# A fused two-block transformer kernel: zero multiplies on TensorE ahead of split features and variance squares, and modulation rows gathered in three batches

## The reference

```python
for l in range(DEPTH):                               # first block
    m_lat = (jax.nn.silu(c) @ ada_w[l] + ada_b[l])[:, None]
    m_ctx = jax.nn.silu(c_ctx) @ ada_w[l] + ada_b[l]
    sh1, sc1, g1, sh2, sc2, g2 = jnp.split(m_lat, 6, axis=-1)
    h_lat = rmsnorm(x, norm_g[l, 0]) * (1.0 + sc1) + sh1
    ...
    x = x + g1 * rmsnorm(y_lat, norm_g[l, 1])
    f_lat = swiglu(rmsnorm(x, norm_g[l, 2]) * (1.0 + sc2) + sh2, ffn_w_in[l], ffn_w_out[l])
    ...
for i in range(DEPTH):                               # second block
    x = layer_norm(DN_ALPHA * x + 0.5 * swiglu_2(x, ...), ...)
    y = mixer_ab(x, ...) if i % 2 == 0 else mixer_c(x, ...)
    x = layer_norm(DN_ALPHA * x + y, ...)
    x = layer_norm(DN_ALPHA * x + 0.5 * swiglu_2(x, ...), ...)
    x = x + jax.nn.sigmoid(x @ ple_wg[i] + ple_bg[i]) * (p[i] @ ple_wp[i])
```

## Time and profile before

| what | value |
|---|---|
| median of three executions | 2632.01 us |
| the profiled execution | 2630.2 us |
| its span, first to last instruction | 2628.4 us |
| TensorE busy (multiplies) | 2366.0 us, 90% of the span |
| VectorE, ScalarE, POOL busy | 1277.7, 894.1, 120.1 us |
| mean granted clock of TensorE | 0.945 of full speed |
| chain of waits | TensorE 84%, VectorE 10%, ScalarE 3% |
| weight stream | 346 loads of 1024 KB |

### The profile page before, as it was taken

The page is one execution under the profiler, slowest core; times in us unless marked ns, Lnnn a source line. Parts: engine busy times, 40 slices in busy tenths (PEclk is TensorE's granted clock), DMA queues, the critical chain, the costliest instruction groups (busy, mean ns, idle before and its releaser), DMA issues.

```text
span 2628.4 us, 39106 instructions
## 1 busy us (share of the span) xinstructions
PE 2366.0 (90%) x17300; PEld 2181.0 (83%) x17300; DVE 1277.7 (49%) x1457; ACT 894.1 (34%) x929; POOL 120.1 (5%) x68
## 2 busy tenths in 40 slices
PE   7988888998899788999799878998899898888997
PEld 5876755998899556999799868998799795878996
DVE  4246425554454243544544545544554586526444
ACT  4212313334333132333433334333333434124332
POOL 0037400000000000000000000000000020000000
PEclk9988998999999999999899989999899996999998
DMA  7246701554355121355355313543354350013451
GB/s 304 98 164 262 289 16 60 180 188 160 133 187 177 71 88 64 144 184 184 128 185 177 129 69 126 188 176 142 130 186 181 108 182 16 1 66 135 177 188 35
DMA packets 52481, 373.10 MB, mean 142 GB/s; under 512 B 5728, under 2 KB 6752, under 8 KB 7840
## 3 DMA queue, kind: packets, MB, share of 16 engines
q1 hardware_dynamic: 51584, 367.78, 38.4%
q0 software_dynamic: 800, 3.93, 0.4%
HBM read 370.64 MB, written 1.05 MB: 141 GB/s over the span
## 4 chain that ended last, share of the span: by engine, by line
PE 84%; DVE 10%; ACT 3%; POOL 1%; issue 1%; DMA 1%; SPq 0%; DVEq 0%; ACTq 0%; POOLq 0%
PE PS L342 10%; PE PS L343 10%; PE PS L344 10%; PE PS L189 7%; PE PS L357 6%; PE PS L356 6%; PE PS L355 6%; PE PS L298 4%; PE PS L645 2%; DVE ring_r L443 2%; PE PS L280 2%; PE PS L263 2%; PE PS L265 2%; PE PS L264 2%; PE PS L281 2%; PE PS L282 2%
## 5 line engine op out<-in xcount | busy, mean ns | idle before, releaser
L443 DVE TENSOR_TENSOR ring_r<-ring,AR_r 128x2048 fp32r<-128x2048 f32 x274 | 625.0, 2289 | 605.8 <-ACT AR_r L437 595.4
L437 ACT ACTIVATE AR_r<-ring 128x2048 fp32r<-128x2048 f32 x274 | 520.1, 1908 | 705.4 <-PE PS L357 306.2
L342 PE MATMUL PS<-AR_r 128*128 128x256 f32 x2240 | 635.3, 284 | 0.0
L343 PE MATMUL PS<-AR_r 128*128 128x256 f32 x2240 | 634.7, 283 | 0.0
L344 PE MATMUL PS<-AR_r,ring_r 128*128 128x256 f32 x2240 | 634.6, 283 | 0.0
L342 PEld LDWEIGHTS PS<-AR_r 128*128 128x128 f32 x2240 | 430.9, 192 | 0.0
L343 PEld LDWEIGHTS PS<-AR_r 128*128 128x128 f32 x2240 | 430.9, 192 | 0.0
L344 PEld LDWEIGHTS PS<-AR_r,ring_r 128*128 128x128 f32 x2240 | 430.9, 192 | 0.0
L355 PE MATMUL PS<-AR_r 128*128 128x256 f32 x1232 | 348.7, 283 | 0.0
L356 PE MATMUL PS<-AR_r 128*128 128x256 f32 x1232 | 348.7, 283 | 0.0
L357 PE MATMUL PS<-AR_r,ring_r 128*128 128x256 f32 x1232 | 348.6, 283 | 0.0
(11 more groups left out here) (346 smaller groups left out, 3290.8 us busy)
## 6 DMA issues: line engine op xcount, KB each, us to landing
ring<-stream SPq DMA_DIRECT2D x346, 1024.0 KB, 4.8
X<-xt SPq DMA_DIRECT2D x1, 2048.0 KB, 10.1
AR<-bias POOLq DMA_DIRECT2D x1, 1536.0 KB, 6.8
AR<-pt POOLq DMA_DIRECT2D x2, 512.0 KB, 3.8
out<-X SPq DMA_DIRECT2D x1, 1024.0 KB, 4.8
SM<-small SPq DMA_DIRECT2D x1, 545.0 KB, 4.1
AR<-invc SPq DMA_DIRECT2D x1, 512.0 KB, 15.3
X<-negl POOLq DMA_DIRECT2D x1, 512.0 KB, 4.0
```

The lines of the kernel that those rows point to most:

```text
L342: pe.matmul(o, w_hi, X_HI[:, k, :], start=(k == 0), stop=False)
L343: pe.matmul(o, w_hi, X_LO[:, k, :], start=False, stop=False)
L437: act.activation(W_HI[i % 3], ring[:, n % SLOTS, :], ACT.Identity).then_inc(split_hi, 1)
L443: dve.tensor_tensor(RING_R[:, n % SLOTS, :], ring[:, n % SLOTS, :], W_HI[i % 3], ALU.subtract).then_inc(split_lo, 1)
```

## The change

It has two parts.

1. `pe_idle_turns` multiplies the zero tile by itself (128 x 128, float32, start and stop) a number of times into a bank that the next work overwrites. 24 such multiplies stand at the head of `pe_chunks_as_features_come`, ahead of its waits, for every tag but `ffn4`; that is nine places: `ffn0_lat`, `ffn0_ctx`, `ffn1_lat`, `ffn2`, `ffn3`, `ple2`, `mix3_in`, `ffn5`, `ple3`. Six stand in `pe_norm` ahead of its first wait for six tags (all in `pe_layernorm`).
2. The 24 groups of modulation are gathered in three batches (4, 8 and 12 groups), each in one PSUM bank: a group's columns of `CS` are shifted by a window so that its two results land on rows of their own, and all groups of a batch accumulate. One copy by ScalarE and one turn (4 multiplies with 8, 16 or 24 columns) serve a batch. The copies and turns of the single groups go: 24 copies become 3, 24 turns become 3.

```diff
@@ pe_norm
             bank = norm_bank(cols) if bank is None else bank
+            if tag in ("ffn2", "mix2", "ffn3", "ffn4", "mix3", "ffn5"):
+                pe_idle_turns(pe, bank, 6)
             for k in range(DT):
...
@@ modulation
-        ada_bank = lambda g: g % 3
+        ADA_BATCHES = [range(0, ADA_FIRST), range(ADA_FIRST, 12), range(12, ADA_GROUPS)]
...
         def pe_ada_rows(pe, g):
+            b = batch_of(g)
+            row = 2 * (g - ADA_BATCHES[b][0])
+            if row == 0:
+                pe.matmul(PS[:, b, 0:2], ZERO[:, :], ZERO[:, 0:2], start=True, stop=False, skip_group_check=True)
             for c in range(2):
...
                 need_chunk(pe, n)
-                if g >= 3 and c == 0:
-                    pe.wait_ge(S["ada_taken"], S.at("ada_taken", g - 3))
                 for k in range(DT):
                     strip = slice(32 * (k % 4), 32 * (k % 4) + 32)
-                    ins = pe.matmul(PS[strip, ada_bank(g), c * T:(c + 1) * T], CS[:, k, :], ring[:, n % SLOTS, k * 256:(k + 1) * 256],
-                                    start=(k < 4), stop=(k >= 4), tile_position=(0, 32 * (k % 4)))
+                    ins = pe.matmul(PS[strip, b, c * T:(c + 1) * T], CS[:, k, 30 - row:62 - row], ring[:, n % SLOTS, k * 256:(k + 1) * 256],
+                                    start=False, stop=(ends_batch(g) and k >= 4), skip_group_check=True, tile_position=(0, 32 * (k % 4)))
...
-        def pe_ada_turn(pe, g):
-            pe.wait_ge(S["ada_taken"], S.at("ada_taken", g))
+        def pe_ada_turn(pe, b):
+            pe.wait_ge(S["ada_taken"], S.at("ada_taken", b))
+            n = len(ADA_BATCHES[b])
+            turned = PS[:, bank, at:at + 8 * n].rearrange("p (g j s) -> p g j s", j=4, s=2)
             for j in range(4):
-                ins = pe.matmul(PS[:, bank, at + 2 * j:at + 2 * j + 2], MODROW[:, g % 2, j * P:(j + 1) * P], SEL[:, :],
+                ins = pe.matmul(turned[:, :, j, :], MODROW[:, b % 2, j * P:(j + 1) * P], SEL[:, 0:2 * n].rearrange("p (g s) -> p g s", s=2),
                                 start=True, stop=True)
...
+        def pe_idle_turns(pe, bank, turns):
+            for _ in range(turns):
+                pe.matmul(PS[:, bank, 0:P], ZERO[:, :], ZERO[:, :], start=True, stop=True)
+
         def pe_chunks_as_features_come(pe, tag, chunks, banks):
+            if tag != "ffn4":
+                pe_idle_turns(pe, banks[0], 24)
...
@@ pe_mix0
             for g in EARLY_GROUPS:
                 pe_ada_rows(pe, g)
-                if g > ADA_FIRST:
-                    pe_ada_turn(pe, g - 1)
...
                 for g in LEVEL_GROUPS[i]:
                     pe_ada_rows(pe, g)
-                    pe_ada_turn(pe, g - 1)
-            pe_ada_turn(pe, ADA_GROUPS - 1)
+                    if g == ADA_BATCHES[2][0]:
+                        pe_ada_turn(pe, 1)
+            pe_ada_turn(pe, 2)
@@ act_mix0
-            for g in EARLY_GROUPS:
-                act_ada(act, g)
             for i, (lv, d) in enumerate(STEPS):
                 act.wait_ge(S["level_exponents"], S.at("level_exponents", i))
                 act.activation(E2[:, i % 2, :], E2[:, i % 2, :], ACT.Exp).then_inc(S["level_decay"], S.mark("level_decay", i))
-                for g in LEVEL_GROUPS[i - 1] if i else ():
-                    act_ada(act, g)
-            for g in LEVEL_GROUPS[-1]:
-                act_ada(act, g)
+                if i and ADA_BATCHES[1][-1] in LEVEL_GROUPS[i - 1]:
+                    act_ada(act, 1)
+            act_ada(act, 2)
```

More of the change, by code:

```diff
@@ L127, in build @@
         M8 = sb("M8", [P, 2 * LEVELS * 256], U8)
-        SEL = sb("SEL", [P, 2])
+        SEL = sb("SEL", [P, 32])
         MOD = sb("MOD", [P, 96, 2])
@@ L166, in build @@
         MODROW = arena(21760, 2, 512)
-        CS = arena(22784, DT, 32)
+        CS = arena(22784, DT, 62)
         HIDDEN = arena(23808, 2, 2 * T)
@@ L224, in build @@
         LEVEL_GROUPS = [range(ada_at(i), ada_at(i + 1)) for i in range(2 * LEVELS)]
+        ada_chunk = lambda g: START["ada_first"] + 2 * g if g < ADA_FIRST else START["ada_rest"] + 2 * (g - ADA_FIRST)
+        batch_of = lambda g: next(b for b, gs in enumerate(ADA_BATCHES) if g in gs)
+        ends_batch = lambda g: any(g == gs[-1] for gs in ADA_BATCHES)
         def pe_ada_rows(pe, g):
+            b = batch_of(g)
+            row = 2 * (g - ADA_BATCHES[b][0])
+            if row == 0:
+                pe.matmul(PS[:, b, 0:2], ZERO[:, :], ZERO[:, 0:2], start=True, stop=False, skip_group_check=True)
@@ L238, in pe_ada_rows @@
                 ins.then_inc(multiplied, 1)
[L240 to L242 removed]
+        def pe_ada_turn(pe, b):
+            pe.wait_ge(S["ada_taken"], S.at("ada_taken", b))
+            bank, at = (5, 0) if b == 0 else (3, 8 * (ADA_BATCHES[b][0] - ADA_FIRST))
+            n = len(ADA_BATCHES[b])
+            turned = PS[:, bank, at:at + 8 * n].rearrange("p (g j s) -> p g j s", j=4, s=2)
@@ L243, in pe_ada_turn @@
             for j in range(4):
-                ins = pe.matmul(PS[:, bank, at + 2 * j:at + 2 * j + 2], MODROW[:, g % 2, j * P:(j + 1) * P], SEL[:, :],
+                ins = pe.matmul(turned[:, :, j, :], MODROW[:, b % 2, j * P:(j + 1) * P], SEL[:, 0:2 * n].rearrange("p (g s) -> p g s", s=2),
                                 start=True, stop=True)
[L246 to L253, removed]
+            ins.then_inc(S["ada_turned"], S.mark("ada_turned", b))
@@ L255, in pe_chunk_split, with act_ada @@
+        def act_ada(act, b):
+            need_product(act, ada_chunk(ADA_BATCHES[b][-1]) + 1)
+            if b >= 2:
+                act.wait_ge(S["ada_turned"], S.at("ada_turned", b - 2))
+            act.activation(MODROW[:, b % 2, :], PS[:, b, :], ACT.Identity).then_inc(S["ada_taken"], S.mark("ada_taken", b))
         def pe_chunk_split(pe, tag, i, bank):
@@ L854, in dve_mix0 @@
             take(len(STEPS) - 1)
-            dve.wait_ge(S["ada_turned"], S.at("ada_turned", ADA_GROUPS - 1))
+            dve.wait_ge(S["ada_turned"], S.at("ada_turned", 2))
             take_modulation(dve, order, 3, 16, 96)
@@ L1833, in _ @@
                 pe_ada_rows(pe, g)
-                if g:
-                    pe_ada_turn(pe, g - 1)
-            pe_ada_turn(pe, ADA_FIRST - 1)
+            pe_ada_turn(pe, 0)
             pe_mix0(pe)
@@ L1890, in _ @@
             act.wait_ge(S["strips_cleared"], S.at("strips_cleared"))
-            act.activation(CS[:, :, 0:2], sm("cvec").rearrange("p (k s) -> p k s", s=2), ACT.Silu).then_inc(S["cond_silu"], S.mark("cond_silu"))
+            act.activation(CS[:, :, 30:32], sm("cvec").rearrange("p (k s) -> p k s", s=2), ACT.Silu).then_inc(S["cond_silu"], S.mark("cond_silu"))
             act_ln_exp(act)
@@ L1899, in _ @@
                 act_rinv(act, order, ("mix0", s), STREAM[s], 0)
-            for g in range(ADA_FIRST):
-                act_ada(act, g)
+            act_ada(act, 0)
             act_mix0(act, order)
@@ L1967, in _ @@
             dve.memset(CS[:, :, :], 0.0).then_inc(S["strips_cleared"], S.mark("strips_cleared"))
-            dve.memset(SEL[:, :], 0.0).then_inc(order.sem, order.step())
             dve.wait_ge(S["consts_loaded"], S.at("consts_loaded"))
-            dve.wait_ge(order.sem, order.n)
             for q in range(4):
-                strip = slice(32 * q, 32 * q + 2)
+                strip = slice(32 * q, 32 * q + 32)
                 dve.tensor_copy(SEL[strip, :], IDENT[strip, strip]).then_inc(S["selector"], S.mark("selector", q))
@@ L1995, in _ @@
                     dve.tensor_tensor(SQ[:, pair(q), STREAM[s]], X[:, pair(q), STREAM[s]], r, ALU.mult).then_inc(S["scaled"], S.mark("scaled", (("mix0", s), q)))
-            dve.wait_ge(S["ada_turned"], S.at("ada_turned", ADA_FIRST - 1))
+            dve.wait_ge(S["ada_turned"], S.at("ada_turned", 0))
             take_modulation(dve, order, 5, 0, 16)
```

3 lines of the change are left out of this document (1 added, 2 removed).

## The result

| | before | changed |
|---|---|---|
| median of the runs, us | 2635.03 (2630.17 to 2641.66, 4 runs) | 2614.29 (2614.01 to 2619.39, 4 runs) |
| profiled execution: time / span / granted clock | 2630.2 / 2628.4 / 0.945 | 2619.39 / 2617.5 / 0.953 |

The ratio is 0.9924, 95% interval 0.9897 to 0.9952: about 0.8% faster. The forecast was 2616 (2607 to 2626).

The account below looks back on a forecast made before the run. TensorE was taken to bound the kernel: full-clock work, gaps at stage joins, and half-clock work behind them. From 2630.2: -10.4 (loop) + 0.9 (ahead of it) + 1.0 (first groups) - 5.6 (joins) gave 2616 us, range 2607 to 2626.

Parts of the forecast that it names:

- Level loop: Without turns, steps take 5.48 us at first, then 6.1 as POOL and VectorE exclude each other: 10.4 us won.
- Rival 1: In the level loop TensorE's pace holds, without exclusion: 15.4 us won instead of 10.4, total 2611; chance 0.12.
- Rival 2: Level loop keeps most of its length, TensorE possibly falling to half clock while waiting: gain 5, total 2622; chance 0.18.
- Ahead of the loop: Without early turns the diagonal products (L632) run at half clock, delaying POOL's first exponents: 0.9 us lost (0 to 1.5).
- First four groups: At the start, ScalarE's copy stands bare, one turn follows, last rows perhaps at half clock: 1.0 us lost.
- Joins: Zeros ahead of stages' first split products remove half-clock stretches at seven joins, but cost 5.4 at mix3_in: 5.6 us won.
- The price of a burst: At the joins, 24 zero multiplies are 48 records and take 5.4 us (5.3 to 5.7) at full clock.
- Rivals 3 and 4: Zeros don't hold the clock, kernel slower: 2644, chance 0.05; zeros end before the wait does, also at ffn3: 2622, chance 0.04.
- The median: Whole kernel: runs' median is 1.8 us above the profiled run, attributed to half-clock stretches the change removes; nothing added.

Follow-up runs that it names:

- e2: The change with only the modulation batches, without `pe_idle_turns` and its calls: 2621.94 us, ratio 0.9918 to before.
- e3: The change without the 24 zero multiplies at mix3_in: 2614.29 us.
- e4: The change without the six zero multiplies in `pe_norm`: 2614.55 us.
- e9: The change with VectorE's two loop multiplies taking a broadcast PSUM column as second operand instead of keys and queries in SBUF: 2606.68 us (2 runs).
- e1: The kernel before with only the zero multiplies added, modulation rows as before: 2633.51 us, ratio 0.9957.
- e8: The change with each zero burst sized to its wait, mix2_in added, none at mix3_in, 36 ahead of its logits: 2603.42 us, ratio 0.9854 to before.
- e7: The change with VectorE's two multiplies per loop step made copies with one SBUF input, products with keys and queries left out: 2610.35 us.
- e12: The change with 48 zero multiplies instead of 24 at ffn3, ple2, ffn5 and ple3: 2637.4 us, ratio 0.9976 to before.

## Why the prediction held, and where its steps were off

- **Level loop, -10.4 predicted.** Measured -10.8 (96.5 against 85.7) in e2, e3 and e4; the change's own profile has only -5.9, since its second product too ran at half clock. The pieces hold as well: in e4 TensorE's own pace is 5.56 to 5.70 (5.48 predicted) for four steps, one of them with the turn, then 5.9 to 6.06 for eight (6.1). The mechanism, POOL and VectorE shutting each other out, is what e9 takes away alone. Rival 1's 15.4 would have been had without it: 14.5 with e9. The prediction saw no other case of exclusion in the loop before; it missed the one just ahead of it, VectorE's first multiply, 2.74 us from 216.16. Rival 2's loss of clock in later steps did not come; with the batches there was none, also in steps where TensorE waited 0.4 us. A reason for that no run tested.
- **Ahead of the loop, +0.9.** It came to 0. The diagonal products did fall to half clock for part of their time (5.2 to 5.8 us; 7.1 predicted), but POOL was busy with other work until then: its first exponents start at 212.43 in the change and 210.37 before, the 2.05 between them being there since 62 us.
- **First four groups, +1.0.** The marks at 62 us read 2.0, -0.4, 0.2 and 1.7, the last without any batch. Over the twelve profiles with batches they lie between -0.8 and 3.3, 1.0 in the mean. That mean is what was predicted, but with two traces without batches to set it against, 0 and 1.7, no effect of the change can be told from scatter between executions, of a size that I had no row for.
- **Joins.** ffn0_lat 0.7 (0.8 predicted), ffn0_ctx 1.5 (1.6), ffn3 1.7, ple2 1.8, ffn5 1.9 (1.7 each), ple3 1.6 in the change's profile, ffn2 0, mix3_in -5.36 (-5.4). ffn1_lat is the one that was off, 3.1 instead of 1.8. The price of a burst, 5.4, measured 5.28 to 5.36. Rivals 3 and 4 are out: the clock at the first split product behind the zeros was 1.00, and the zeros ran as long as priced.
- **What I left out** are the neighbours. Of ffn1_lat's 3.1, 1.4 came at the sums ahead of it, where less was at half clock; ffn0_ctx handed back 1.0 at its first down product (L384) and 0.6 at mix1, ffn2 and mix2 0.9; mix3 behind the zeros gave 2.1 to 2.4. The stretches at half clock that come after a burst shift, worth 0.6 to 5 us either way. Here the neighbours nearly cancelled: from the first zeros on the gain is 7.3 in e1 and 7.1 in the change, against 5.6, and most of the rest is ffn1_lat's 1.3. In e3 and e8 they did not cancel.
- **The median.** I took before's spread for stretches behind gaps that the zeros would remove. It is there in e1 with zeros (2624 to 2635) and gone in e2 without them, so it went with what the batches replaced, most likely the turns in the loop. So 2632.01, the median of three runs that I was shown, was kind to before; by all 48 it is 2641, and the gain 1.0%.
- **How much of it was luck.** The mechanisms held, but that the sum came within 2 us owes something to chance. Ahead of the loop 0.9 less was lost than predicted, the loop gave 0.4 more and the joins 1.5 more; the start, 2.0 in the change's profile instead of 1.0, gave 1.0 of these 2.8 back, by scatter. And the sum was taken from a profiled execution of before that is one of its quickest: against the median of its 48 runs the gain is 27 us, not the 16 of the forecast.
- In the Trainium skill, "SBUF — State Buffer", section "Who interferes with whom", a VectorE instruction with two inputs in SBUF and a GpSimd instruction that reads SBUF exclude each other. The trace agrees in every late step, 3.0 us where 1.2 and 2.0 stand alone, and e9, with one input moved to PSUM, agrees from the other side.

## What to carry to other kernels

Multiplying zeros in a wait buys the half-clock stretch behind it, 1.5 to 2 us here, and costs 0.11 us a record beyond the wait: size each burst by its own wait, put it ahead of the wait and not behind it, and leave it out where the queue goes on at once. Check the whole chain behind a burst, since later stretches at half clock shift (5.2 us handed back in e3 and e8). Where small instructions are taken out of a loop, look at which pair of engines comes next: here an operand in PSUM instead of SBUF was worth 3.8 us in the loop. e9 left the real operand out, so what bringing it to PSUM costs was not measured.

## What was unexpected in the hardware

- A float32 copy on VectorE from SBUF to SBUF (0.68 us) waits out POOL's TENSOR_TENSOR as a two-input multiply does, ending 0.55 us behind it; a multiply with one input in SBUF and one in PSUM does not (1.21 us beside it), nor did the predicated copies from PSUM (1.4 us for four).
- TensorE's granted clock fell to half inside the old loop while TensorE never idled (e1: products of 4.63 and 6.93 instead of 3.62 us; the change took the turn of eight records out of all steps but one, and no such fall was seen in twelve profiles). Why was not settled.
- The stage behind mix3_in, the same code in twelve of the kernels, takes 253.4 to 253.9 us in seven profiles (the change, e1, e4 to e7, e9), 254.6 in e12, 255.8 in two and 258.9 in two, with 39 to 56 us of it at half clock. What chooses was not settled.
